# Differential attention's values unit by unit in a shared PSUM bank, short convolutions in halves, three projection groups and their turns moved, filter taps paired: a two-block transformer kernel

## Chip, cores and metric

One core of a Trainium2 chip runs the whole program. The metric is the device time of one execution in microseconds; the kernel before takes 1582.85 us (median of 3 runs, 1582.10 to 1583.59).

## The reference, cut to what matters

Two blocks follow each other on 512 tokens of width 1024. The first has a stick-breaking attention, a pooled and a gated branch and a feed-forward of width 4096. The second, which the change is about, mixes two parts and then has a gated feed-forward (width 2816):

```python
# differential attention, 4 heads, queries 512, keys 256 (context) + 512
s = einsum("bhmqd,bhmkd->bhmqk", q, k) * (64 ** -0.5)      # m: 2 maps of a head
a = softmax(s, axis=-1)
w = a[:, :, 0] - lam * a[:, :, 1]
o = einsum("bhqk,bhkd->bhqd", w, v)                        # then rmsnorm(o) * (1 - lam_init)
# hyena mixer, three parts of width 512: v, x1, x2
u = short_conv(hx @ w_hy)                                  # 3 taps along the tokens
z = v
for n, gate in enumerate((x1, x2)):
    z = gate * (long_conv(z, k_f[:, n]) + skip[n] * z)     # by a transform, a product, its inverse
# the filters k_f: three sine layers of width 64 and one linear layer, once for all tokens
```

## The kernel before, in words

Every product of an activation with a weight is made from split numbers: a value is a high part and a low part in the type fp32r, and three matmuls (high by high, low by high, high by low) stand for one (`mm3`). Weights come in units of 128 x 1024. SP issues their DMAs into four raw buffers, ACT copies a unit to its high part (line 1081), and DVE (line 1651) or, for the units in the list POOL_LOW, POOL (line 2274) subtracts it from the raw values for the low part. Units of the kind "pre" (the transform tables) come already split: POOL issues two DMAs for each (lines 2284, 2285). Small fp32 matmuls have two records each in the trace.

Each engine has one program, written out by hand; it works in its own order and waits on semaphores. The functions with one name on several engines (`diff_turn`, `hyena_turn`, `fold`) are the parts of one step.

**Filters (early, beside the first block's projections).** `filter_layer` makes three sine layers of 64 features; `taps(i, o)` makes two fp32 matmuls with 64 rows of contraction (64 x 512 each, d = 0 and 1), eight times in all; DVE multiplies by the decay, POOL adds and subtracts the two.

**Differential attention.** A unit is one head and 128 queries, 16 units. For unit n:
- PE `diff_scores(n)`: 12 matmuls into banks 0 to 3, two maps side by side on the two halves of the rows.
- DVE `diff_max(n)`: for each map a maximum over 768 keys (line 2062) and a product by -0.125 (line 2064).
- ACT `diff_scores(n)`: for each map the exponential (line 1444), scale 0.125.
- DVE `diff_weights(n)`: reciprocal, factor (line 2074) and the difference of the maps (line 2076).
- PE `diff_turn(n)`: six transposes into banks 4 and 5; ACT copies them to WT (line 1435).
- PE `diff_values(h)`, after the four units of a head: six fp32 matmuls with 512 columns into the free one of banks 6 and 7; ACT evicts O2F (line 1424), DVE then S2F (line 2055), ACT squares it.

Between these PE puts the hyena projections: `hyena_part(j, part)`, 6 matmuls, two parts in each step of the loop, groups j = 0 to 7 into banks 6 and 7 (RING2). ACT writes the convolution's middle tap (`conv_center`, line 1452), DVE adds the other two in six steps (`hyena_conv`, line 2083). In step n PE does scores(n), sometimes values, turn(n-2), two parts.

**Behind it.** PE does turns 0 to 3 of the convolved groups, group 8 with its projection, turns 4 to 7, `sub_sums` (sums of squares for the attention's norm, 16 matmuls of one column, 32 records), group 9 and turn 8. ACT evicts the turns to U (line 1475). `fold(o)` adds and subtracts halves of U (DVE line 2114, high parts ACT line 1481, low parts DVE line 2117 and POOL line 2417). Then for each order o = 0, 1: `forward(o, f)`, f = 0 to 3 (12 matmuls each), `spectral` (DVE: four products at line 2158, then lines 2160 and 2162; ACT the high and POOL the low part), and `backward(o, f)` (12 matmuls each). Turns 9 to 11 and `sub_scale(h)` stand between them. Group 10 stands ahead of backward(0, 2), group 11 after backward(0, 3), beside the gating (DVE lines 2177, 2181), and fold(1) comes next. The forwards take their banks in turn from 0 to 3 (RING4), and a bank is free when its last reader is done. After backward(1, 3) PE starts on w_out_2 (`wide2`) with the attention's half of the input, while ACT and DVE gate and norm the hyena half.

`mm` and `bank` are at lines 431 to 446, PE's loop over the units at about 895 to 935.

## Time and profile before

| what | value |
|---|---|
| median of 3 runs | 1582.85 us |
| the profiled execution | 1580.21 us |
| its span | 1578.5 us |
| PE busy | 1507.5 us (96%), 6878 matmul records |
| DVE busy | 877.3 us (56%) |
| ACT busy | 622.5 us (39%) |
| POOL busy | 291.1 us (18%) |
| mean granted TensorE clock | 0.991 |

The span is the profiled part of the execution; 1.7 us lie around it. A busy time is a share of the whole span and says nothing of a single stage. Matmul records overlap: the time from the start of one to the start of the next is what a matmul costs, and its own duration is longer.

### The profile page before, as it was taken

The page shows a single profiled execution, that of the slowest core. Times are in us where ns is not written, and L with a number is a line of the kernel's source. Part 1 is how long each engine was busy: PE and PEld are TensorE (multiplying, and loading weights), DVE is VectorE, ACT ScalarE, POOL GpSimd, SP SyncE. Part 2 cuts the span into 40 slices and gives each one's busy share as a digit, 9 for nine tenths or more (in the row PEclk, how much of TensorE's full clock was granted, in tenths as well). Part 3 has the DMA queues.
Part 4 walks back from the last instruction along what each step waited for, and adds up shares of the span by engine and source line. Part 5 has one row for each costly group of instructions (what it writes and reads, how often), then busy time and mean ns, then how long its engine had stood idle before and what let it go on. Part 6 is the DMA issues. An engine that isn't in the chain of part 4 may idle for free.

```text
span 1578.5 us, 17718 instructions
## 1 busy us (share of the span) xinstructions
PE 1507.5 (96%) x6878; PEld 1200.0 (76%) x6878; DVE 877.3 (56%) x1429; ACT 622.5 (39%) x978; POOL 291.1 (18%) x289
## 2 busy tenths in 40 slices
PE   6999999999989999999997998989798999999998
PEld 5767667888868878888886876668576888888886
DVE  5445556555467654565447438856766455334534
ACT  5535664222353322334335325644344333223332
POOL 0253111110122200122004310006441110111101
PEclk9999999999999999999999999999999999999999
DMA  7342002654345544545326221124442322323221
GB/s 232 126 146 81 27 28 93 235 166 148 132 134 173 174 147 140 178 145 178 113 100 208 91 67 40 41 94 139 131 154 69 108 93 95 99 89 106 94 94 54
DMA packets 53262, 187.87 MB, mean 119 GB/s; under 512 B 6104, under 2 KB 6616, under 8 KB 52986
## 3 DMA queue, kind: packets, MB, share of 16 engines
q1 hardware_dynamic: 47386, 165.76, 32.3%
q0 software_dynamic: 4736, 16.78, 3.2%
q10 hardware_dynamic: 1056, 4.19, 0.7%
q8 instruction: 55, 0.90, 0.2%
q14 instruction: 29, 0.24, 0.0%
HBM read 174.12 MB, written 12.58 MB: 118 GB/s over the span
## 4 chain that ended last, share of the span: by engine, by line
PE 80%; DVE 9%; issue 4%; ACT 4%; POOL 3%; DMA 0%; SPq 0%; DVEq 0%; POOLq 0%; ACTq 0%
PE PS L447 79%; POOL TMP L2311 2%; DVE smallring L2062 1%; DVE TMP L2083 1%; PE PS L458 1%; ACT em L1444 1%; DVE wl L1651 1%; DVE TMP L2158 1%; DVE em L2076 1%; POOL y L2321 0%; DMA X<-in_x 0%; ACT wh L1081 0%; DVE accm L1631 0%; ACT wt L1435 0%; POOL wl L2274 0%
## 5 line engine op out<-in xcount | busy, mean ns | idle before, releaser
L1651 DVE TENSOR_TENSOR wl<-raw,wh 128x1024 fp32r<-128x1024 f32 x219 | 283.8, 1299 | 283.1 <-ACT wh L1081 283.0
L447 PE MATMUL PS<-HTh,wh 128*128 128x512 f32 x1056 | 419.7, 397 | 12.4 <-DVE TMP L1977 5.8
L447 PE MATMUL PS<-HTh,wl 128*128 128x512 f32 x1056 | 413.0, 391 | 0.0
L447 PE MATMUL PS<-HTl,wh 128*128 128x512 f32 x1056 | 412.8, 391 | 0.0
L1081 ACT ACTIVATE wh<-raw 128x1024 fp32r<-128x1024 f32 x228 | 239.1, 1053 | 286.2 <-PE PS L447 251.9
L447 PEld LDWEIGHTS PS<-HTh,wh 128*128 128x128 f32 x1056 | 199.5, 189 | 61.3 <-issue 11.0
L447 PEld LDWEIGHTS PS<-HTh,wl 128*128 128x128 f32 x1056 | 199.0, 188 | 42.8
L447 PEld LDWEIGHTS PS<-HTl,wh 128*128 128x128 f32 x1056 | 199.5, 189 | 38.5 <-issue 0.5
L447 PE MATMUL PS<-wh,FFh 128*128 128x512 f32 x432 | 169.1, 392 | 0.0
L447 PE MATMUL PS<-wh,FFl 128*128 128x512 f32 x432 | 168.2, 389 | 0.0
L447 PE MATMUL PS<-wl,FFh 128*128 128x512 f32 x432 | 168.1, 389 | 0.0
L1631 DVE SCALAR_TENSOR_TENSOR accm<-raw,small,accm 128x256 f32<-128x256 f32 x224 | 108.0, 516 | 3.4
L2234 DVE SCALAR_TENSOR_TENSOR TMP<-PS,pp,TMP 128x255 f32<-128x255 f32 (+1 forms) x132 | 52.1, 395 | 80.3 <-ACT TMP L1583 76.4
L447 PEld LDWEIGHTS PS<-wh,FFl 128*128 128x128 f32 x432 | 81.1, 188 | 17.1
L447 PEld LDWEIGHTS PS<-wl,FFh 128*128 128x128 f32 x432 | 81.1, 188 | 16.5
L447 PEld LDWEIGHTS PS<-wh,FFh 128*128 128x128 f32 x432 | 81.1, 188 | 16.5
L2384 POOL TENSOR_TENSOR FFl<-TMP,FFh 128x512 fp32r<-128x512 f32 x32 | 41.6, 1299 | 240.1 <-ACT FFh L1295 240.1
L2466 POOL TENSOR_TENSOR FFl<-TMP,FFh 128x512 fp32r<-128x512 f32 x22 | 28.5, 1294 | 211.8 <-ACT FFh L1590 211.8
L1295 ACT ACTIVATE FFh<-TMP 128x512 fp32r<-128x512 f32 x32 | 20.2, 632 | 66.5 <-DVE TMP L1917 66.5
L1291 ACT ACTIVATE TMP<-PS 128x512 f32<-128x512 f32 x32 | 19.0, 595 | 57.7 <-PE PS L447 57.7
L2083 DVE SCALAR_TENSOR_TENSOR TMP<-PS,pp,TMP 128x255 f32<-128x255 f32 (+1 forms) x72 | 28.4, 395 | 16.0 <-ACT TMP L1452 13.9
L2474 POOL TENSOR_TENSOR X<-X,TMP 128x512 f32<-128x512 f32 x14 | 19.7, 1434 | 90.1 <-DVE TMP L2249 90.1
(320 smaller groups left out, 2163.7 us busy)
## 6 DMA issues: line engine op xcount, KB each, us to landing
raw<-in_ws SPq DMA_DIRECT2D x268, 512.0 KB, 3.8
taps<-TMP SPq DMA_DIRECT2D x16, 256.0 KB, 2.5
tab<-in_spec POOLq DMA_DIRECT2D x8, 512.0 KB, 5.6
raw<-taps SPq DMA_DIRECT2D x8, 512.0 KB, 3.7
kd<-TMP POOLq DMA_DIRECT2D x16, 256.0 KB, 4.3
wh<-in_wd POOLq DMA_DIRECT2D x8, 512.0 KB, 3.9
wl<-in_wd POOLq DMA_DIRECT2D x8, 512.0 KB, 4.6
kf<-kd SPq DMA_DIRECT2D x8, 512.0 KB, 3.9
```

The source lines that it names most:

```text
L447: return nc.tensor.matmul(out, l, r, start=start, stop=stop, skip_group_check=True)
L1081: act(WH[u % SLOTS][:, :n], RAW[i % RAWS][:, :n], ACT.Copy).then_inc(sem("w_hi"), 1)
L1291: act(T(q % 2), PS[:, BANK["ff", hf, m], :], ACT.Relu).then_inc(sem("ff_relu"), 1)
L1295: act(FFh[:, m, :], T(2 + q % 2), ACT.Copy).then_inc(sem("ff_hi"), 1)
L1631: stt(acc, r[:, k % 4, :], c, acc, ALU.mult, ALU.add).then_inc(sem("mod_acc"), 1)
L1651: tt(WL[k][:, :n], RAW[RAW_AT["unit", u, 0] % RAWS][:, :n], f32(WH[k][:, :n]), ALU.subtract).then_inc(sem("lo_dve"), 1)
L2083: stt(out[:, do], ps[:, di], pp("hy_conv_w_2", 12 * w + j), out[:, do], ALU.mult, ALU.add).then_inc(sem("hc_v"), 1)
L2234: stt(z[:, do], ps[:, di], pp("ffn_conv_w_2", 22 * w + m), z[:, do], ALU.mult, ALU.add).then_inc(sem("uc_v"), 1)
L2311: tt(T(k), T(3), T(5), op).then_inc(sem("tap_ed"), 1)
L2384: tt(FFl[:, q % 16, :], T(2 + q % 2), f32(FFh[:, q % 16, :]), ALU.subtract).then_inc(sem("ff_lo"), 1)
L2466: tt(FFl[:, m - first_m, :], T(m % 4), f32(FFh[:, m - first_m, :]), ALU.subtract).then_inc(sem("ug_lo"), 1)
L2474: tt(x, x, T(4 + q % 4), ALU.add).then_inc(sem("dn_xp"), 1)
```

## The change

Nine edits; the diff is cut to its core.
1. PE's taps go in pairs: the filter layers put their 64 features out twice, on partitions 0 to 63 and 64 to 127, w4 is stored as 128 x 1024, and the matmul for d = 1 uses the upper half of the rows.
2. The scale 0.125 moves into q (ACT's high part, DVE's low part), and the maximum is negated by its own instruction; line 2064's 32 instructions go.
3. The attention's values are made per unit, 6 matmuls of 128 columns into columns 256 to 383 of bank 5, the upper one of the transposes' banks; ACT and DVE evict 128 columns, 16 times. The turn of a unit moves one step earlier, and WT has two buffers.
4. `hyena_conv` is done in two halves of three steps, one in each step of the loop.
5. The low parts of the weight units from the fourth hyena group on go to POOL.
6. The turns of groups 0 to 6 stand around the last unit's turn and ahead of its values, turn 7 after them.
7. Group 8 (with its turn) moves behind forward(0, 3), groups 9 and 10 behind backward(0, 3), group 11 between backward(1, 1) and backward(1, 2), its turn after backward(1, 3), before `wide2`.
8. `sub_sums` moves behind forward(0, 0), sub_scale(0) behind forward(0, 1).
9. ACT's eviction of turn 8 (and 11) stands ahead of its two copies of the backward sums.

```diff
-BEFORE = 10
+BEFORE = 8
...
-        if o == 0:
-            pack(colmajor("w_in_2", 1536 + 10 * P, 1))
+        pack(colmajor("w_in_2", 1536 + (8 if o == 0 else 11) * P, 1))
         pack(inv[2] + inv[3], "pre")
         if o == 0:
-            pack(colmajor("w_in_2", 1536 + 11 * P, 1))
+            pack(colmajor("w_in_2", 1536 + 9 * P, 2))
...
 POOL_LOW = [u for u in range(NU) if u not in PRE and (
-    AT["dft_f", 0, 0][0][0] + SLOTS - 1 <= u < AT["w_out_2", 0, 0][0][0] + SLOTS - 1
+    AT["w_in_2", 0, 1536][0][0] + SLOTS - 1 <= u < AT["w_out_2", 0, 0][0][0] + SLOTS - 1
...
+                for d in range(2):
+                    pr = slice(64 * d, 64 * d + 64)
+                    mm(PS[:, BANK["tap", n + d], :], TMP[pr, 4, i * P:(i + 1) * P], W4[pr, o * S:(o + 1) * S], True,
+                       True).then_inc(sem("p_tap"), 1)
...
-            def diff_values(h):
-                b = bank(("dv", h), "dv_ev", h + 1, (13 - BANK["hy", (ahead - 1) // 4],))
+            def diff_values(n):
+                h, _ = DIFF[n]
+                BANK["dv", n] = b = TPAIR[0] + 1
                 e.wait_ge("v2_ev", 3)
                 e.wait_ge("v2_evv", 3)
-                e.wait_ge("wt_ev", 4 * h + 4)
+                e.wait_ge("wt_ev", n + 1)
+                drained[b] = ("dv_ev", n + 1)
                 for k in range(6):
-                    i = mm(PS[:, b, :], V2[:, k, h * P:(h + 1) * P], WT[:, k, :], k == 0, k == 5)
+                    i = mm(PS[:, b, 256:384], V2[:, k, h * P:(h + 1) * P], WT[n % 2][:, k, :], k == 0, k == 5)
...
+            for n in range(len(DIFF) + 1):
+                if n < len(DIFF):
+                    diff_scores(n)
+                else:
+                    for j in TURN_AT[0]:
+                        hyena_turn(j)
+                if n:
+                    diff_turn(n - 1)
+                if n < len(DIFF):
+                    for part in range(2):
+                        hyena_part(n // 2, n % 2 * 2 + part)
+                else:
+                    for j in TURN_AT[1]:
+                        hyena_turn(j)
+                if n:
+                    diff_values(n - 1)
+            hyena_turn(7)
...
             for o in range(2):
                 for f in range(4):
                     forward(o, f)
-                    if f == 0:
-                        if o:
-                            hyena_turn(10)
+                    if f == 0 and o == 0:
+                        sub_sums()
+                    if f == 1 - o:
                         sub_scale(3 * o)
-                    if f == 3:
-                        hyena_turn(9 + 2 * o)
-                        if o == 0:
-                            sub_scale(1)
+                    if f == 3 and o == 0:
+                        sub_scale(1)
+                    if f in (1, 2) and o:
+                        hyena_turn(8 + f)
                     if f >= 2:
                         backward(o, f - 2)
-                if o == 0:
-                    hyena_group(10)
+                hyena_group(8 + 3 * o)
                 backward(o, 2)
                 backward(o, 3)
+                hyena_turn(8 + 3 * o)
                 if o == 0:
-                    hyena_group(11)
+                    hyena_group(9)
+                    hyena_group(10)
                     sub_scale(2)
...
+            for n in range(len(DIFF) + 1):      # VectorE
                 if n < len(DIFF):
                     diff_max(n)
+                if n > 1:
+                    if n < len(DIFF):
+                        hyena_conv(n // 2 - 1, range(3 * (n % 2), 3 * (n % 2) + 3))
+                    else:
+                        hyena_conv(7)
+                        fold(0, (0, 1))
                 if n < len(DIFF):
                     diff_weights(n)
+                    weights(unit("w_in_2", 0, 1536 + n // 2 * P) + SLOTS - 1)
+                if n:
+                    diff_values(n - 1)
...
+            for n in range(len(DIFF) + 1):      # ScalarE
+                if n > 1:
+                    diff_values(n - 2)
+                if n == len(DIFF):
+                    for j in TURN_AT[0]:
+                        hyena_turn(j)
+                if n:
+                    diff_turn(n - 1)
+                if n < len(DIFF):
+                    diff_scores(n, 0)
+                    diff_scores(n, 1)
...
+            diff_values(len(DIFF) - 1)
```

In order 1 VectorE does hyena_conv(10) behind spectral(4) and sub_high(3), ahead of spectral(5); hyena_conv(8) and hyena_conv(11) stand ahead of its wait for the last backward, hyena_conv(9) behind fold(1) and sub_high(2).

## Rows read from the trace of the kernel before

**Rows 1.** Windows: us, busy (records) of PE, PEld, DVE, ACT, POOL, clock, DMA
```profile
60.00:130.00 70.00, 70.00 (x272) 49.72 (x272) 32.36 (x37) 27.49 (x36) 35.64 (x31) 1.00 0.45 141
950.11:1057.21 107.10, 95.53 (x504) 68.26 (x505) 81.67 (x166) 56.19 (x97) 1.13 (x2) 1.00 0.18 55
1106.86:1129.34 22.48, 12.99 (x46) 7.56 (x44) 17.73 (x31) 6.71 (x13) 7.78 (x8) 0.90 0.45 145
1129.34:1153.43 24.09, 21.04 (x89) 16.99 (x89) 17.12 (x21) 9.30 (x14) 18.63 (x12) 0.95 0.28 88
```

**Rows 2.** Waits of PE, 950 to 1160: releaser, us in total, times, longest
```profile
PE PS L447 <- ACT em L1444: 7.8, 9, 1.0
```

**Rows 3.** Timeline of PE, one unit: start, us, instructions
```profile
993.23 0.50 PE L447 MATMUL PS<-KTh,QTh 64*128 64x512 f32 x2
994.48 0.87 PE L458 MATMUL PS<-cst,em 128*128 128x128 f32 x6
995.11 0.48 PE L447 MATMUL PS<-HTh,wh 128*128 128x512 f32 x1
...
998.10 0.50 PE L447 MATMUL PS<-KTh,QTh 64*128 64x512 f32 x2
```

**Rows 4.** Groups of DVE by line: busy us, mean ns of one
```profile
L2062 DVE TENSOR_REDUCE smallring<-PS 128x1 f32<-128x768 f32 x32 | 30.4, 951 | 0.0
L2064 DVE TENSOR_SCALAR smallring<-smallring 128x1 f32<-128x1 f32 x32 | 4.9, 154 | 1.1
L2076 DVE SCALAR_TENSOR_TENSOR em<-em,smallring,em 128x768 f32<-128x768 f32 x16 | 16.3, 1019 | 0.6
```

**Rows 5.** Timeline of DVE, one low part and one whole convolution
```profile
953.59 1.21 DVE L1651 TENSOR_TENSOR wl<-raw,wh 128x1024 fp32r<-128x1024 f32 x1
958.30 2.54 DVE L2083 SCALAR_TENSOR_TENSOR TMP<-PS,pp,TMP 128x255 f32<-128x255 f32 x6
```

**Rows 6.** Timeline of PE, a head's values and the turn behind them
```profile
977.55 5.42 PE L447 MATMUL PS<-wt,V 128*128 128x512 f32 x12
982.81 0.82 PE L458 MATMUL PS<-cst,em 128*128 128x128 f32 x6
```

**Rows 7.** Timeline of PE, fp32 matmuls of 1 and of 128 columns
```profile
1066.22 3.63 PE L447 MATMUL PS<-cst,s2f 128*128 128x1 f32 x32
144.66 1.09 PE L447 MATMUL PS<-wst,bc 128*64 128x128 f32 x16
```

**Rows 8.** Groups of ACT by line: busy us, mean ns of one
```profile
L1444 ACT ACTIVATE em<-PS,smallring 128x768 f32<-128x768 f32 x32 | 28.6, 901 | 6.6 <-DVE smallring L2064 6.3
L1435 ACT ACTIVATE wt<-PS 128x768 f32<-128x768 f32 x16 | 12.9, 809 | 17.4 <-PE PS L458 17.4
L1487 ACT ACTIVATE ndg<-cst,small 128x128 f32<-128x128 f32 x16 | 5.1, 390 | 0.0
```

**Rows 9.** Timeline: POOL's low part of a unit and DVE beside it
```profile
1139.82 2.84 POOL L2274 TENSOR_TENSOR wl<-raw,wh 128x1024 fp32r<-128x1024 f32 x1
...
1140.33 2.88 DVE L2162 TENSOR_TENSOR TMP<-TMP 128x512 f32<-128x512 f32 x1
```

**Rows 10.** Timeline of PE, 1107 to 1130: the stretch behind the first gating
```profile
1115.12 0.47 PE L447 MATMUL PS<-EDh,wh 128*128 128x512 f32 x1 [1.80 <-issue]
1126.95 2.07 PE L447 MATMUL PS<-ndg,cst 128*128 128x512 f32 x2 [5.01 <-DVE TMP L2083]
1129.34 0.79 PE L447 MATMUL PS<-EDh,wh 128*128 128x512 f32 x1 [0.32 <-DVE TMP L2158]
```

**Rows 11.** Windows of 1 us: the clock behind sub_sums and behind the gap
```profile
1072.00:1073.00 1.00, 1.00 (x4) 0.80 (x3) 0.00 (x0) 0.00 (x0) 0.00 (x0) 0.50 0.77 193
1127.00:1128.00 1.00, 1.00 (x2) 0.45 (x2) 1.00 (x2) 0.00 (x0) 0.00 (x0) 0.50 1.13 410
```

**Rows 12.** Timeline of PE: a step of four tap records and what follows
```profile
65.16 1.98 PE L447 MATMUL PS<-w,TMP 64*128 64x512 f32 x4
67.07 0.50 PE L447 MATMUL PS<-HTh,wh 128*128 128x512 f32 x1
```

More of the change, by code:

```diff
@@ L919, in hyena_part @@
                     i.then_inc(sem("p_hy"), 1)
[L921 to L932 removed]
             RING4, ACC = (0, 1, 2, 3), (4, 5, 6, 7)
             def hyena_group(j):
[L938 removed]
+                bank(("hy", j), "hc_v", 6 * j + 6, ACC if j == 10 else RING4)
                 for k in KT:
@@ L1385, in rotated @@
                 dh = QTh[:, r, :] if r < 4 else KTh[:, r - 4, 256:]
-                act(dh, T(2 + r % 3), ACT.Copy).then_inc(sem("qk2_hi"), 1)
+                act(dh, T(2 + r % 3), ACT.Copy, **({"scale": 0.125} if r < 4 else {})).then_inc(sem("qk2_hi"), 1)
             for m in range(4):
@@ L1492, in sub_high @@
                 act(O2h[:, h, :], NO2[:, :], ACT.Copy).then_inc(sem("o2_hi"), 1)
[L1494 to L1495 removed]
             fold(0)
[L1497 to L1506 removed]
+            diff_squares(3)
+            hyena_turn(7)
             def spectral(n):
@@ L1518, in scalar_program @@
                     spectral(4 * o + f)
-                    if f == 0:
-                        if o:
-                            hyena_turn(10)
+                    if f == 0 and o == 0:
+                        e.wait_ge("sub_v", 4)
+                        act(SUBR[:, 16:32], SUBR[:, 16:32], ACT.Sqrt, scale=2.0 ** -8,
+                            bias=1e-6 * 2.0 ** -8).then_inc(sem("sub_rt"), 1)
+                        sub_diag(0)
+                    if f == 1 - o:
                         sub_high(3 * o)
@@ L2050, in vector_program, with fold, fold_low, diff_values @@
             ts(SUBG, pp("subln_2"), 1.0 - lam_init, None, ALU.mult).then_inc(sem("lam_v"), 1)
-            def diff_values(h):
-                e.wait_ge("dv_o", h + 1)
-                ts(S2F[:, h, :], PS[:, BANK["dv", h], :], 2.0 ** 64, -2.0 ** 64, ALU.min, ALU.max).then_inc(sem("dv_ev"), 1)
+            def fold(o, cs):
+                for c in cs:
+                    i = c % 2
+                    if o == 0:
+                        e.wait_ge("u_ev", 4)
+                        e.wait_ge("p_ht", c + 3)
+                    else:
+                        for t in (i, i + 2):
+                            e.wait_ge(*Z_READY(0, t))
+                        e.wait_ge("z_p", 1)
+                    tt(T(2 + c), U[:, i, 0:512], U[:, i + 2, 0:512], ALU.add if c < 2 else ALU.subtract).then_inc(sem("fd_v"), 1)
+            def fold_low(o, c):
+                e.wait_ge("ed_hi", 4 * o + c + 1)
+                tt(EDl[:, c, :], T(2 + c), f32(EDh[:, c, :]), ALU.subtract).then_inc(sem("ed_lo"), 1)
+            def diff_values(n):
+                h, qb = DIFF[n]
+                e.wait_ge("dv_o", n + 1)
+                ts(S2F[:, h, qb * P:(qb + 1) * P], PS[:, BANK["dv", n], 256:384], 2.0 ** 64, -2.0 ** 64, ALU.min,
+                   ALU.max).then_inc(sem("dv_ev"), 1)
             def diff_max(n):
@@ L2119, in sub_high, with spectral @@
+                if n:
+                    diff_values(n - 1)
             def sub_high(h):
                 e.wait_ge("p_sn", h + 1)
-                e.wait_ge("dv_o", h + 1)
+                e.wait_ge("dv_o", 4 * h + 4)
                 e.wait_ge("o2_lo", h)
                 tt(NO2[:, :], O2F[:, h, :], PS[:, BANK["sn", h], :], ALU.mult).then_inc(sem("sn_v"), 1)
-            fold(0)
-            weights(unit("w_in_2", 0, 1536 + 8 * P) + SLOTS - 1)
-            hyena_conv(8)
+            def spectral(n):
+                kf = KF[n % 2]
+                br, bi = PS[:, BANK["fw", n, 0], :], PS[:, BANK["fw", n, 1], :]
+                k0, k2 = 2 + 2 * (n % 2), 3 + 2 * (n % 2)
+                e.wait_ge("p_fw", n + 1)
+                e.wait_ge(f"d_kf{n % 2}", 16 * (n // 2 + 1))
+                if n >= 2:
+                    e.wait_ge("ys_lo", 2 * (n - 2) + 2)
+                e.wait_ge("pr_v", 6 * n)
+                for k, x, c in ((k0, br, 0), (6, bi, 1), (k2, br, 1), (7, bi, 0)):
+                    tt(T(k), x, kf[:, c, :], ALU.mult).then_inc(sem("pr_v"), 1)
+                e.wait_ge("pr_v", 6 * n + 2)
+                tt(T(k0), T(k0), T(6), ALU.subtract).then_inc(sem("pr_v"), 1)
+                e.wait_ge("pr_v", 6 * n + 4)
+                tt(T(k2), T(k2), T(7), ALU.add).then_inc(sem("pr_v"), 1)
@@ L2129, in vector_program @@
+            fold_low(0, 0)
+            fold(0, (2, 3))
+            fold_low(0, 2)
+            spectral(0)
             ps, fits, r, q = PS[:, BANK["sub"], 0:16], SUBR[:, 0:16], SUBR[:, 16:32], SUBR[:, 32:48]
```

235 lines of the change are left out of this document (78 added, 157 removed).

## The prediction

> **What bounds the kernel now.** I read the windows by stage first. From 60 to 130 us PE is busy without a break, although POOL and DVE work beside it; there a microsecond less of PE is a microsecond less of time. The differential attention (950.11 to 1057.21) has 107.1 us and 95.5 of PE, and the stretch from the first gating to the last backward has 22.5 us with 13.0 of PE and 24.1 with 21.0 [rows 1]. So 11.6 + 9.5 + 3.1 = 24.2 us of PE are idle in the part that is rebuilt, and this is all that a new order alone can bring.
>
> What PE waits for in the attention is ACT's exponential, 9 times, about 1 us each [rows 2]. The cause lies one engine back. A unit without values costs PE 998.10 - 993.23 = 4.87 us: scores 1.25, turn 0.63, two projection parts 2.99 [rows 3]. DVE's unit is longer: two maxima and two scalings 2 x (0.95 + 0.15) = 2.2, reciprocal, factor and difference about 1.5 (1.02 the difference) [rows 4], half a convolution 1.27 and half a low part 0.6 [rows 5], together 5.5 to 5.6. DVE sets the pace for three units, and in the fourth PE is alone for 982.81 - 977.55 = 5.26 us with a head's values [rows 6] while DVE has no work. The two limits add up instead of covering each other.
>
> Behind the gating PE starts forward(1, 0) at 1115.12, waits 5.01 us for a convolution, and reaches forward(1, 1) only at 1129.34 [rows 10].
>
> **The sum, part by part**, against the profiled 1580.2 us (2.6 below the median of 1582.85).
>
> *Taps.* A step has four records of 0.43 and takes PE 67.07 - 65.16 = 1.91 us [rows 12]. Two matmuls on different halves of the rows can run side by side, as the two maps' scores do (rows of x2, [rows 3]), but the two records of one fp32 matmul use the same rows. In the order A, A, B, B only the second A and the first B overlap: three slots for four, 8 x 0.43 = 3.4 us. Bounds: 0 (no overlap) and 6.9 (both overlap). I take 3.4. The doubled features change no column count, so the filter layers cost nothing more; POOL's tap chain has slack beside PE [rows 1].
>
> *Values.* Before: 4 x 5.26 = 21.0. After: 16 x 12 records of 128 columns. With one column a record costs 3.63 / 32 = 0.113 us, the pace of loading 128 weight columns; at 512 columns it costs 0.43, so 128 columns stream in 0.107 [rows 6, 7]. If load and stream overlap, a record costs 0.115 and a unit 1.4, with the change of shape 1.5: 24.0, so 3.0 more than before. Bounds: 0.107 and, one after the other, 0.22. I take 0.115, because the 12 records at 0.43 show their loads wholly hidden.
>
> *Pace of a unit.* PE: 4.87 + 1.5 = 6.37 us. DVE: maxima 1.9 (negation costs nothing), 1.5, half a convolution 1.27, a small eviction 0.3, no low part: 5.0. ACT: 0.81 + 2 x (0.90 + 0.20) + half of 0.77 and of 1.05 + 0.39 = 4.3 [rows 8]. The ring scores, maximum, exponential, exponential, scores is 1.25 + 0.1 + 0.96 + 0.95 + 1.1 + 0.2, about 4.6, and the ring from a turn by the copy of WT, two exponentials and the weighting to the next turn about 5.2. All are under 6.37, so PE runs through. The tightest place: turn(n) may not write bank 5 before DVE has evicted values(n-1), PE's last work of the step before. That takes 0.2 + 0.4 + 0.3 + 0.1 = 1.0 us, and scores(n) cover 1.25. First wait as before (0.5), then 949.85 + 6.75 + 14 x 6.37: step 16 starts at 1045.8.
>
> *From there to backward(0, 3).* Turns, the last turn and values need 5.85 us. fold(0) then is bare, for group 8 no longer covers it: ACT evicts seven turns and one unit first, and the last low part is ready 11.8 later, so forward(0, 0) ends at +12.4, 3.8 of that idle. Then sub_sums 3.6, three forwards and four backwards 7 x 2.75, two sub_scale 1.9, group 8 5.5, and about 2 us in which sub_scale(0) waits for the norm's chain (DVE, ACT's root, ACT's diagonal), now begun behind spectral(0): +45.1, 1090.9. DVE's work of spectral(0), 3.9, is hidden by sub_sums and forward(0, 1).
>
> *Order 1.* ACT evicts turn 8 first, so gating and fold(1) are 1.1 later; groups 9 and 10 (11 us) fill what was idle. forward(1, 0) ends at +14.8, sub_scale(3) at +16.1. Then banks and DVE decide: forward(1, 1) gets the banks of group 9 and of forward(1, 0), and waits 0.8 for spectral(4); forward(1, 2) gets one of forward(1, 1), and spectral(5) stands behind sub_high(3) and convolution 10 (0.7 + 2.54), so it waits 3.6 more. Then two forwards, four backwards and group 11 run through: +47.0, 1137.9, and turn 11 0.5: `wide2` starts at 1138.4 and not at 1153.4, **15.0 us earlier**. Its own cover of 10.9 us is longer than the gating and norm behind it, 1.1 later.
>
> *Clock.* It falls to 0.50, the 1.2 GHz level, behind sub_sums and behind the gap in order 1 [rows 11]; eight matmuls at 0.43 for 0.23 in the first case. Sparse stretches stay (turns, bare fold, sub_sums, the wait before forward(1, 2)). I take 2 us; bounds 0 and 5.
>
> *The rest.* q's scale is in operations that are there; the later low parts lie on an idle POOL; the DMAs keep their order; each pre unit is issued over 4 us ahead of its use.
>
> Sum: 3.4 + 15.0 - 2 = 16.4 us. 1580.2 - 16.4 = 1563.8 for the profiled execution, **1566.4 for the median**.
>
> **Rules against it.** The 12 value records on the full array, 0.43 us apart for 512 columns, leave no room for a load between them [rows 6]. The Trainium skill (TensorE: Matmul & The Clock Gate, The mechanism) says that a weight load overlaps running matmuls only where the row group differs; these records all use the whole array, so by the rule their loads would lie bare. By that rule (rival 1) the time is 1587; the rows speak against it.
>
> POOL's low part at 1139.82 lasts 2.84 us, and a DVE subtraction issued at 1140.33 takes 2.88 [rows 9]. The Trainium skill (SBUF — State Buffer, Who interferes with whom) says that a DVE instruction with two SBUF inputs and a GpSimd instruction that reads SBUF shut each other out for the whole instruction. The trace agrees; this is rival 4.
>
> **Rivals.**
> 1. *The value records pay load and stream one after the other*, 0.113 + 0.107 = 0.22: 192 x 0.105 = 20.2 us more, 1586.6, slower than before. Place: the end of each unit on PE. For it: nothing in the trace has fp32 records of 128 columns over 128 weight columns back to back. Against it: 16 records of 128 columns and 64 weight columns in 1.09 us, 0.054 apart, two column halves at a time [rows 7]. It decides from 0.20 a record (16.4 / 192 = 0.085 over 0.115). 5%.
> 2. *The shared bank sets the pace.* If ACT or DVE is 1 us late with the eviction of values(n-1), each turn stalls: 15 us over 15 units, 1581, no change. For it: the margin is 0.25 us; against it: both have over 1 us of free time in each unit. 7%.
> 3. *The moved groups leave as much bare as they cover.* Fold and norm chain cost 5 more in order 0, spectral(4) to (6) 3 more in order 1: 1574. For it: a chain over four engines, scheduled by hand from single rows. 11%.
> 4. *POOL's port.* Five low parts (2.4 each) now lie beside DVE's difference of the maps, which has two SBUF inputs. If POOL starts first, turn(n) is late by 2.4 less 1.2 of slack, five times 1.2: 6 us, 1572. Against it: POOL waits for ACT's copy (1.05), which starts with DVE's own release, so DVE comes first. 9%.
>
> **How the numbers follow.** My forecast has 68%. About 0.2% (3.2 us) is what a measurement can tell from no change. Faster: 68 + 11 + 9 = 88%; same: rival 2, 7%; slower: rival 1, 5%. Range: lower end with full overlap of the taps (-3.5), no clock loss (-2) and half of the 9 us of remaining waits gone (-4): 1557; upper end takes in rivals 3 and 4 and no gain from the taps: 1576.
>
> **What would show it.** Value records 0.11 to 0.12 us apart; about 6.4 us from scores to scores; no line 2064; PE's waits for line 1444 gone except at the start. A pace over 6.8 with DVE's S2F eviction as releaser is rival 2, records at 0.22 rival 1. Four tap records in about 1.5 us. `wide2` some 18 us earlier, PE idle about 4 us ahead of forward(0, 0) and about 4 ahead of forward(1, 2)'s second half. If the attention, without the turns put into it, does not get shorter by some 9 us, or the stretch behind it by 5, the forecast is wrong there.

## The result and the profile after

The kernel after takes **1556.42 us** (median of 4 runs, 1555.44 to 1558.83), the kernel before 1582.59 us beside it (4 runs, 1582.1 to 1583.59): a ratio of 0.9836, 95% interval 0.9821 to 0.985. I had forecast 1566.4 with a range of 1557 to 1576. The sign and the places were right; the time lies 10 us under the forecast and 0.6 under the range. The profiled execution took 1555.44 us with a span of 1553.7, against 1578.5 before: 24.8 us less where I had summed 16.4.

The page of the kernel after: busy time of each engine, and the groups of low parts on POOL and on DVE.

```profile
PE 1501.7 (97%) x7022; PEld 1211.4 (78%) x7022; DVE 866.1 (56%) x1402; ACT 626.1 (40%) x990; POOL 307.7 (20%) x296
...
L1658 DVE TENSOR_TENSOR wl<-raw,wh 128x1024 fp32r<-128x1024 f32 x212 | 274.4, 1299 | 282.4 <-ACT wh L1087 282.1
L2287 POOL TENSOR_TENSOR wl<-raw,wh 128x1024 fp32r<-128x1024 f32 x16 | 40.2, 2512 | 114.1 <-ACT wh L1087 114.1
```

PE is busy 5.8 us less than before with 144 records more, the 192 value records of 128 columns for 48 of 512. Against 24.8 us of span that is a quarter: the rest was idle time. POOL's line 2287 has 16 low parts of 128 x 1024, against 9 before.

The waits of PE from 950 to 1160 in the kernel after, as [rows 2] (releaser, us in total, times, longest).

```profile
PE PS L448 <- DVE TMP L2147: 3.6, 2, 3.2
PE PS L448 <- issue: 2.0, 2, 1.3
PE PS L448 <- DVE no L2134: 1.3, 2, 0.9
PE PS L448 <- DVE EDl L2076: 1.1, 1, 1.1
```

The exponential's line is gone from that list. The timeline of PE in the kernel after: a step of taps, as [rows 12]; a unit, as [rows 3]; the last unit's end and the fold; order 1 up to `wide2`, as [rows 10].

```profile
63.31 1.13 PE L448 MATMUL PS<-w,TMP 64*128 64x512 f32 x4
64.37 0.50 PE L448 MATMUL PS<-HTh,wh 128*128 128x512 f32 x1
...
937.97 0.49 PE L448 MATMUL PS<-KTh,QTh 64*128 64x512 f32 x2 [1.98 <-DVE V L2045]
...
955.26 0.50 PE L448 MATMUL PS<-KTh,QTh 64*128 64x512 f32 x2
...
957.13 0.48 PE L448 MATMUL PS<-HTh,wh 128*128 128x512 f32 x1
...
959.95 1.50 PE L448 MATMUL PS<-wt,V 128*128 128x128 f32 x12
961.38 0.50 PE L448 MATMUL PS<-KTh,QTh 64*128 64x512 f32 x2
...
1034.72 1.47 PE L459 MATMUL PS<-cst,TMP 128*128 128x128 f32 x12
...
1041.69 0.47 PE L448 MATMUL PS<-EDh,wh 128*128 128x512 f32 x1 [1.32 <-issue]
...
1044.83 0.47 PE L448 MATMUL PS<-EDh,wh 128*128 128x512 f32 x1 [1.07 <-DVE EDl L2076]
...
1105.25 0.79 PE L448 MATMUL PS<-EDh,wh 128*128 128x512 f32 x1 [3.18 <-DVE TMP L2147]
...
1129.10 0.47 PE L448 MATMUL PS<-wh,O2h 128*128 128x512 f32 x1 [0.73 <-issue]
```

The four tap records take 64.37 - 63.31 = 1.06 us, where they took 1.91. The attention starts at 937.97, 7.1 us earlier than before (945.03); eight steps of 0.85 are 6.8 of it. A unit takes 961.38 - 955.26 = 6.12 us, values included. `wide2` starts at 1129.10, 24.3 us earlier than before (1153.43). So nearly all of the gain lies ahead of `wide2`. The windows of the stretches in the kernel after, as [rows 1] (us, busy time and records of PE, PEld, DVE, ACT, POOL, granted clock, DMA).

```profile
937.97:1034.72 96.75, 96.09 (x654) 82.14 (x655) 72.42 (x142) 59.12 (x111) 16.10 (x9) 1.00 0.19 61
1034.72:1079.35 44.63, 41.30 (x208) 33.07 (x207) 32.97 (x54) 23.14 (x44) 25.97 (x21) 0.96 0.39 122
1079.35:1129.10 49.75, 44.47 (x189) 34.76 (x188) 34.05 (x57) 19.03 (x32) 29.70 (x23) 0.97 0.46 153
```

In the attention (the first row) PE is idle for 0.7 us of 96.8; in the two stretches behind it for 3.3 and 5.3 us.

### The profile page after: what moved, and what is told of

It is laid out like the page before. It is cut to its first block, busy times and chain, and to the rows that moved or that the text cites. A ratio compares the mean times of both kernels' runs of the same rounds, so it can differ in the third digit from the quotient of the medians.

```text
span 1553.7 us, 18006 instructions
## 1 busy us (share of the span) xinstructions
PE 1501.7 (97%) x7022; PEld 1211.4 (78%) x7022; DVE 866.1 (56%) x1402; ACT 626.1 (40%) x990; POOL 307.7 (20%) x296
## 4 chain that ended last, share of the span: by engine, by line
PE 86%; DVE 5%; issue 3%; POOL 3%; ACT 2%; DMA 0%; SPq 0%; POOLq 0%; DVEq 0%; ACTq 0%
PE PS L448 85%; PE PS L459 2%; POOL TMP L2324 2%; DVE wl L1658 1%; DVE TMP L2147 0%; POOL y L2334 0%; DVE TMP L1711 0%; DMA X<-in_x 0%; ACT wh L1087 0%; DVE accm L1638 0%; DVE HTl L1974 0%; DVE TMP L2110 0%; ACT TMP L1367 0%; DVE Y L1863 0%; DVE TMP L1904 0%
## 5 line engine op out<-in xcount | busy, mean ns | idle before, releaser
L1658 DVE TENSOR_TENSOR wl<-raw,wh 128x1024 fp32r<-128x1024 f32 x212 | 274.4, 1299 | 282.4 <-ACT wh L1087 282.1
L2247 DVE SCALAR_TENSOR_TENSOR TMP<-PS,pp,TMP 128x255 f32<-128x255 f32 (+1 forms) x132 | 52.1, 395 | 79.3 <-ACT TMP L1590 75.4
L2287 POOL TENSOR_TENSOR wl<-raw,wh 128x1024 fp32r<-128x1024 f32 x16 | 40.2, 2512 | 114.1 <-ACT wh L1087 114.1
```

What stands on the lines that cost most here:

```text
L1658: tt(WL[k][:, :n], RAW[RAW_AT["unit", u, 0] % RAWS][:, :n], f32(WH[k][:, :n]), ALU.subtract).then_inc(sem("lo_dve"), 1)
L2247: stt(z[:, do], ps[:, di], pp("ffn_conv_w_2", 22 * w + m), z[:, do], ALU.mult, ALU.add).then_inc(sem("uc_v"), 1)
L2287: tt(WL[k][:, :n], RAW[RAW_AT["unit", u, 0] % RAWS][:, :n], f32(WH[k][:, :n]), ALU.subtract).then_inc(sem("lo_pool"), 1)
```

## The experiments

The groups e1 to e4; e5, e6, f1, f2; f3, g1, g2, h1; k0 to k3; and m1, m2 each shared a chip and its runs of the kernel before; ratios are to those. The unchanged kernel after gave medians of 1556.42, 1555.87 and 1558.03 on three occasions, and in the profiled executions of k0 to k3, m1 and m2 the attention started anywhere from 937.5 to 941.4, with the same code ahead of it. Differences of under 3 us are therefore read from a stretch of the trace, not from the medians. Two stretches serve: from the first scores to step 16, the step behind the last scores (96.75 us in the kernel after), and from step 16 to `wide2` (94.38).

**The taps alone (e1), and everything but the taps (e2).** e1 is the kernel before with edit 1, e2 the kernel after without it.

```diff
+                for d in range(2):
+                    pr = slice(64 * d, 64 * d + 64)
+                    mm(PS[:, BANK["tap", n + d], :], TMP[pr, 4, i * P:(i + 1) * P], W4[pr, o * S:(o + 1) * S], True, True)
```

> Edit 1 alone on the kernel before: the two taps of a step stand on the two halves of the rows, nothing else changed. Theory 1 (drawn from the profile after, where four tap records end in 1.13 us and the attention starts 7.1 us earlier): both records of one matmul run beside both of the other, two slots for four, so 8 steps x 2 x 0.43 = 6.9 us less than the kernel before: a ratio of 0.9956. Rival (the prediction's own term): only the second record of the first and the first of the second overlap, 3.4 us less, 0.9978. Second rival: the tap chain on the vector and GpSimd engines sets the pace there, 0 to 2 us less.

> The kernel after without edit 1: taps one after the other on the upper 64 rows, the rest of the change left in. Theory 1: the parts add up, so the time is that of the kernel after plus 6.9 us, 1563.3, a ratio of 0.9878 to the kernel before, and the attention and what is behind it account for the other 19 us. Rival: the parts share a bound (the saving before the attention is partly eaten by a later wait), then it is above after by 3.4 or less (1559.8, 0.9856).

e1: 1573.99 us, a ratio of 0.9957 (0.994 to 0.9974), 6.8 us by the ratio. e2: 1564.74, 0.9893 (0.9878 to 0.9907), and its span is 1561.6, 7.9 us over the kernel after. A step of e1 on PE:

```profile
63.76 1.13 PE L447 MATMUL PS<-w,TMP 64*128 64x512 f32 x4
64.81 0.50 PE L447 MATMUL PS<-HTh,wh 128*128 128x512 f32 x1
```

1.05 us for four records of 512 columns, two slots of 0.43 and the change of shape (before, 1.91 for four slots and it): not three slots. The parts add up. My term of 3.4 was half of what the taps bring.

**Value records twice (e5).** The kernel after with each unit's six value matmuls issued twice into one accumulation.

```diff
-                for k in range(6):
+                for k in [*range(6), *range(6)]:
```

> The kernel after, with each unit's value matmuls issued twice into the same accumulation (12 more records of 128 columns a unit; the attention's output is then doubled, so the outputs differ from the reference's). Theory 1: the tensor engine alone sets the pace, and a record costs 0.113 to 0.12 us, load and stream overlapped: 192 x 0.115 = 22 us more than the kernel after (1578.5, 0.9974). Rival (the prediction's rival 1, load and stream one after the other) 0.22 each, 42 us more (1598.5, 1.010). Third: other engines' slack is what sets the pace and takes part of it up, under 18 us more.

1579.19 us, 0.9976 (0.9966 to 0.9986), 22.8 us over 1556.42. Two units on PE:

```profile
958.30 0.50 PE L448 MATMUL PS<-KTh,QTh 64*128 64x512 f32 x2
...
963.03 2.84 PE L448 MATMUL PS<-wt,V 128*128 128x128 f32 x24
965.80 0.50 PE L448 MATMUL PS<-KTh,QTh 64*128 64x512 f32 x2
```

A unit takes 7.50 us and not 6.12: 1.38 / 12 = 0.115 us a record, and no other engine takes any of it up. Load and stream one after the other would have been 0.22. Rival 1 of the prediction is out, and PE alone sets the pace of the attention.

**Convolutions whole (e4), low parts back on DVE (e3), both (g1).** Edits 4 and 5 undone in the kernel after, singly and together.

```diff
-                        hyena_conv(n // 2 - 1, range(3 * (n % 2), 3 * (n % 2) + 3))
+                        if n % 2 == 0:
+                            hyena_conv(n // 2 - 1)
...
-    AT["w_in_2", 0, 1536][0][0] + SLOTS - 1 <= u < AT["w_out_2", 0, 0][0][0] + SLOTS - 1
+    AT["dft_f", 0, 0][0][0] + SLOTS - 1 <= u < AT["w_out_2", 0, 0][0][0] + SLOTS - 1
```

> The kernel after, with the low parts of the weights that ride in the attention subtracted on the vector engine again, as in the kernel before (five or so of them, 1.2 us each). Theory 1: the vector engine has 70 us of work in the 92 us of the attention, and 6 more leave it under the tensor engine's pace; only the eviction that the next unit's turn waits for comes late, some 0.55 us in four or five units, so 2.7 us more than the kernel after (1559.1, 0.9852). Rival A: the queue hides it, 0 to 0.5 us more. Rival B (the prediction's rival 4, the port shared by GpSimd and the vector engine): the moved low parts cost the kernel after something, and undoing the move gains 1 to 6 us.

> The kernel after, with each short convolution of the attention whole in every second unit (2.54 us on the vector engine at once) and not in halves of 1.27 in each. Theory 1: a unit with a whole convolution has 6.3 us of work for the vector engine and the next one 3.8; the tensor engine's 6.12 is passed only just, and the turn that waits for the eviction is late by 0.4 us in seven units: 2.8 us more than the kernel after (1559.2, 0.9852). Rival: the slack of the queue takes it up, 0 to 0.5 us more.

> The kernel after with both: convolutions whole in every second unit, and the low parts of the weights of the attention on the vector engine. e4 (whole convolutions alone) took 9 us more than the kernel after, where 2.8 were expected; in its trace four differences of the maps last 2.9 us and not 1.02, each while GpSimd makes a low part, and the next turn waits 1.8 us. Theory 1: what costs the 9 us is that the longer convolution puts the difference behind GpSimd's start; with the low parts on the vector engine the four waits of 1.8 go, and what is left is the work of 6.3 us in the units with a convolution: 1 to 3 us more than after (1558.5, 0.9848). Rival: it is the vector engine's amount of work that costs, then this kernel, with 1.2 us more of it in every second unit, is slower than e4: 1566 or more (0.990).

e3: 1557.67 us, 0.9846 (0.9831 to 0.9861), 1.3 over the kernel after and within what separates its own measurements; in its trace four turns wait 0.9 us in all for line 2082, and those four units take 6.44 to 6.46 us. e4: 1565.42, 0.9895 (0.988 to 0.991), 9.0 over. g1: 1562.71, 0.9871 (0.9852 to 0.9891), 6.3 over. From the first scores to step 16 the traces have:

| convolutions | low parts on POOL | low parts on DVE |
|---|---|---|
| in halves | 96.75 (after) | 98.41 (e3) |
| whole | 104.19 (e4) | 101.18 (g1) |

So e4 was a miss by a factor of three, and g1, with more work for DVE than e4, is 3.0 us shorter. The cause stands in DVE's timeline. First a unit of the kernel after with POOL's low part beside it, then one of e4 with DVE, POOL and PE.

```profile
954.41 1.02 DVE L2102 SCALAR_TENSOR_TENSOR em<-em,smallring,em 128x768 f32<-128x768 f32 x1
...
954.89 2.78 POOL L2287 TENSOR_TENSOR wl<-raw,wh 128x1024 fp32r<-128x1024 f32 x1 [8.53 <-ACT wh L1087]
```

```profile
966.61 2.54 DVE L2110 SCALAR_TENSOR_TENSOR TMP<-PS,pp,TMP 128x255 f32<-128x255 f32 x6
...
969.27 2.37 POOL L2288 TENSOR_TENSOR wl<-raw,wh 128x1024 fp32r<-128x1024 f32 x1 [11.74 <-ACT wh L1087]
969.57 2.89 DVE L2102 SCALAR_TENSOR_TENSOR em<-em,smallring,em 128x768 f32<-128x768 f32 x1
...
972.71 0.87 PE L459 MATMUL PS<-cst,em 128*128 128x128 f32 x6 [1.76 <-DVE s2f L2082]
```

In the kernel after DVE starts the difference of the maps at 954.41, POOL its low part at 954.89; DVE takes 1.02 us, POOL 2.78 where it takes 2.39 alone. In e4 the longer convolution lets POOL start first, by 0.30 us, and the difference takes 2.89. The next turn waits 1.76 for what DVE does behind it. That happens four times, 7.0 us of waits. In g1 POOL is out of it and four units are 7.22 to 7.25 us long instead of 6.12, those in which a whole convolution (2.54) and a low part (1.2) fall together: 4.1 us of waits, with no low part on POOL beside them. The Trainium skill (SBUF — State Buffer, Who interferes with whom) says that the two instructions shut each other out for their whole length; the trace agrees to within 0.2 us: in e4 the difference ends 0.82 us behind POOL's low part (972.46 and 971.64) and alone takes 1.02. What it means for this change: with convolutions in halves moving the low parts to POOL gains 1.7 us, with whole ones it costs 3.0. The halves keep the difference 0.48 us ahead of POOL.

**The two DVE edits on the kernel before (e6), one of them alone (g2).** e6: edits 2 and 5; g2: edit 2.

```diff
-                    nc.vector.reduce_max(r[:, m:m + 1], s, axis=mybir.AxisListType.X).then_inc(sem("df_mx"), 1)
-                    e.wait_ge("df_mx", 4 * n + 2 * m + 1)
-                    ts(r[:, m:m + 1], r[:, m:m + 1], -0.125, None, ALU.mult).then_inc(sem("df_mx"), 1)
+                    nc.vector.reduce_max(r[:, m:m + 1], s, axis=mybir.AxisListType.X, negate=True).then_inc(sem("df_mx"), 1)
```

> The kernel before with two of the small edits alone: the scaling by -0.125 taken out of the vector engine (the negation in the maximum, the scale in q's split) and the low parts of the weights moved to GpSimd. The values stay with each head. Theory 1: the vector engine's pace was what made the tensor engine wait for the exponentials; its unit falls from 5.5 to about 4.7 us, under the tensor engine's 4.87, so the waits for line 1444 (7.8 us) go and the attention is 7 to 9 us shorter: 1574.5, a ratio of 0.9949. Rival: the waits come back elsewhere (the ring of exponential and scores), 0 to 3 us less, and the placing of the values unit by unit is what brings the attention's gain.

> The kernel before with the scaling by -0.125 taken out of the vector engine alone; the low parts stay on the vector engine. e6 (both) took 9 us more than before: its differences last 2.9 us four times behind GpSimd's low parts, and the tensor engine waits 2.1 us for the exponential behind each. Theory 1: the low parts on GpSimd are the whole of that loss, and the scaling alone brings 0.3 us of the vector engine's time a unit where it sets the pace, 12 units: 1 to 4 us less than before (1579.5, 0.998). Rival: the vector engine isn't what the tensor engine waits for; the same time as before within 0.5 us. Second rival: the denser pace lets the granted clock fall, more than before.

e6: 1591.72 us, 1.0057 (1.0042 to 1.0073): 9 us slower than before, where I expected 8 less. g2: 1578.73, 0.9978 (0.9965 to 0.9991), 3.4 us less. e6 on POOL, DVE and PE:

```profile
972.93 2.39 POOL L2275 TENSOR_TENSOR wl<-raw,wh 128x1024 fp32r<-128x1024 f32 x1 [9.49 <-ACT wh L1081]
973.23 2.91 DVE L2077 SCALAR_TENSOR_TENSOR em<-em,smallring,em 128x768 f32<-128x768 f32 x1
...
979.05 0.58 PE L447 MATMUL PS<-KTh,QTh 64*128 64x512 f32 x2 [2.15 <-ACT em L1444]
...
981.06 6.24 PE L447 MATMUL PS<-wt,V 128*128 128x512 f32 x12
987.13 0.82 PE L458 MATMUL PS<-cst,em 128*128 128x128 f32 x6
```

The same meeting. From the first scores to the turns behind the last values e6 has 121.8 us, the kernel before 112.2. Its whole convolutions put the difference behind POOL's low part in four units, PE's waits for the exponential come to 11.2 us in place of 7.8, and behind the 2.15 us of idle time the granted clock falls (0.83 over 978 to 988): the head's values take 6.07 us and not 5.26. g2 shows that DVE did set the pace before: with 0.3 us less a unit the waits for the exponential fall from 7.8 to 4.0 us. (The profiled execution of g2, 1582.70, is the longest of its ten, so nothing else is read from it.)

**Banks of `wide2` one by one (f1).**

```diff
-            banks0 = [bank(("o2", i), "o2_v", i + 1, RING4) for i in range(4)]
+            banks0 = []
...
+                        if c == 0:
+                            banks.append(bank(("o2", i), "o2_v", i + 1, RING4))
```

> The kernel after, with the output projection (wide2) taking its four banks one by one, each just before its first matmul, and not all four ahead of the first. Theory 1: the 0.73 us idle ahead of it is the wait for the eviction of turn 11, whose bank is one of the four; taken last, it is out of the way: 0.8 to 1.0 us less than the kernel after (1555.5). Rival: that idle time is the issue of the first matmul and stays, 0.

1554.95 us, 0.9829 (0.9805 to 0.9853). From the last step of the attention to `wide2` its trace has 1128.47 - 1035.11 = 93.36 us, the kernel after 1129.10 - 1034.72 = 94.38: 1.0 less, and the 0.73 us of "issue" are gone. They were the wait for ACT's eviction of turn 11.

**Convolution 10 later (f2).**

```diff
-                    if f == 0 and o:
+                    if f == 1 and o:
                         hyena_conv(10)
```

> The kernel after, with convolution 10 behind spectral(5) on the vector engine, and turn 10 behind backward(1, 0) on the tensor engine. Theory 1: the wait of 3.18 us ahead of forward(1, 2)'s second half is for spectral(5), which stands behind convolution 10 in the vector engine's queue; moved, the wait goes and the bank is free 2.5 us earlier: 2.5 to 3 us less than the kernel after (1553.6, 0.9817). Rival: the tensor engine then waits for convolution 10 itself ahead of turn 10, 0 to 1 us less.

1558.45 us, 0.9848 (0.9827 to 0.9868), 95.55 us from step 16 to `wide2` against 94.38: nothing gained. PE in f2:

```profile
1105.24 0.50 PE L448 MATMUL PS<-EDh,wh 128*128 128x512 f32 x1 [0.74 <-DVE TMP L2149]
...
1109.97 0.47 PE L448 MATMUL PS<-ysh,wh 128*128 128x512 f32 x1 [3.07 <-POOL ysl L2447]
```

The wait ahead of forward(1, 2) falls from 3.18 to 0.74 us and one of 3.07 stands ahead of backward(1, 0). The releaser named is POOL's low part of spectral(5), which backward(1, 0) does not read. By the code it is the bank: group 10 is in the ring of backward's four banks, so backward(1, 0) needs convolution 10, which ends at 1109.7 there. Either order waits for the same sum of DVE's work. That the bank holds it is read from the code and these two ends, and was not tested.

**`sub_sums` into the fold's wait (f3).**

```diff
+            sub_sums()
             for o in range(2):
                 for f in range(4):
                     forward(o, f)
-                    if f == 0 and o == 0:
-                        sub_sums()
```

> The kernel after, with sub_sums put ahead of forward(0, 0), into the wait for the fold's low part, the squares of the last head between the fold's high parts on ScalarE, and the norm's chain of small operations ahead of spectral(0). Theory 1: sub_sums (3.5 us) covers the waits of the fold on the tensor engine (1.3 and 1.1 us idle) and the norm's chain is ready before sub_scale(0) asks for it (0.24 us): 2 us less than the kernel after (1554.4, 0.9822). Rival: sub_sums needs the last head's squares, which come only behind the fold's high parts, so the wait is longer ahead of sub_sums instead: 0 to 1 us more than after.

The diff above shows PE's part; on DVE the norm's chain also goes ahead of spectral(0). 1559.09 us, 0.985 (0.9834 to 0.9866), 2.7 over the kernel after, and 97.75 us from step 16 to `wide2`, 3.4 more. PE in f3:

```profile
1042.47 5.43 PE L448 MATMUL PS<-cst,s2f 128*128 128x1 f32 x32 [1.58 <-ACT s2f L1435]
...
1057.99 2.05 PE L448 MATMUL PS<-ndg,cst 128*128 128x512 f32 x2 [2.96 <-ACT ndg L1498]
```

It waits 1.58 us for the last head's squares, its 32 records take 5.43 us and not 3.63 (the granted clock is 0.66 over them, 1.00 in the kernel after), and sub_scale(0) waits 2.96 for the diagonal, which on ACT stands behind spectral(0)'s high parts, now later. The first wait is the rival's mechanism. The low clock and the longer wait, which the move of the norm's chain on DVE brings, were in neither theory.

**Low parts and the spectrum's DMA in order 1 (h1, k2), the fold's low part (k1).** h1 and k2 take POOL's low part at 1096.19 out of DVE's chain; k2 also puts one DMA ahead of another on SP, and sub_low(3) on POOL one spectral step later; k1 moves one low part of each fold from POOL to DVE. The diff has h1's condition first, then k2's edits on POOL and SP, then k1's.

```diff
-                    weights(unit("dft_f", 128, f * P, o) + SLOTS - 1)
+                    if o == 0 or f > 1:
+                        weights(unit("dft_f", 128, f * P, o) + SLOTS - 1)
...
-                    weights(unit("dft_f", 128, f * P, o) + SLOTS - 1)
+                    if n != 4:
+                        weights(unit("dft_f", 128, f * P, o) + SLOTS - 1)
...
-                    if f == 0:
+                    if n in (0, 5):
                         sub_low(3 * o)
...
+                if n == 4:
+                    load_spectrum(6)
                 weights(unit("dft_f", 128, f * P, o) + SLOTS - 1)
-                if n + 2 < 8:
+                if n + 2 < 8 and n != 4:
...
             fold_low(0, 0)
+            fold_low(0, 1)
             fold(0, (2, 3))
```

> The kernel after, with one low part of order 1 (the unit of group 11, 2.4 us on GpSimd at 1096.2, used at 1116.9) done behind the low parts of spectral(5) instead of ahead of those of spectral(4). In the kernel after the vector engine's subtraction at 1097.2 takes 1.92 us beside it and not 0.68, and the vector engine works without a break from there to spectral(5), for which forward(1, 2) waits 3.2 us. Theory 1: the subtraction is back at 0.68 and the wait is 1.2 us shorter: 1.2 us less than the kernel after (1555.2, 0.9827). Rival: another GpSimd operation then meets the vector engine's chain, 0 to 0.5 us less.

> The kernel after, with the low part of group 11's unit behind the low parts of spectral(4) on GpSimd, as in h1, but only by one place, and with the DMA of the spectrum for spectral(6) issued ahead of the raw unit's on SP. In h1 the vector engine waited 13.3 us for that spectrum: its DMA was issued at 1114.67 and not at 1099.00, behind the raw unit's, which waits for the low part that frees its buffer. Theory 1: that queue was the whole of h1's loss; now it is away, and the subtraction of spectral(4) is back at 0.68 us: 1.2 us less than the kernel after. Rival A: the raw unit itself comes late, 2 us or more above after. Rival B: the same as after, another engine ends that stretch.

> The kernel after, with the second low part of each fold made by the vector engine itself (0.6 us) and not by GpSimd, beside which the vector engine's next sums of the fold take 2.39 us for two and not 1.29. Theory 1: shut out for 1.1 us, it gets 0.5 us back in each fold; the tensor engine's wait of 1.07 us for the third low part of the fold falls to 0.5, and order 1 starts 0.5 us earlier: 0.5 to 1.0 us less than the kernel after. Rival: no meeting of the two engines, the sums are slow for another reason; then 0.6 us more in each fold, 0.6 to 1.2 us more than after.

h1: 1568.74 us, 0.9906 (0.9888 to 0.9924), 12 us over the kernel after. DVE and SP in h1:

```profile
1101.30 0.68 DVE L2149 TENSOR_TENSOR TMP<-TMP 128x512 f32<-128x512 f32 x1
...
1114.67 0.91 SPq L2592 DMA_DIRECT2D kf<-kd  x2
...
1122.52 2.48 DVE L2147 TENSOR_TENSOR TMP<-PS,kf 128x512 f32<-128x512 f32 x4 [13.29 <-DMA kf<-kd]
```

The subtraction is back at 0.68 us, as expected, and 13.29 us are lost to a queue that I had not followed: the low part frees a raw buffer, SP waits for that buffer to load the next unit, and the spectrum's DMA stands behind that load. In k2 it stands ahead of it (issued at 1097.00): 1555.45 us, 0.9833 (0.9818 to 0.9847), and 1127.61 - 1034.39 = 93.22 us from step 16 to `wide2`, 1.2 less than the kernel after. k1: 1554.78, 0.9832 (0.9817 to 0.9847), 1127.95 - 1034.20 = 93.75 us, 0.6 less; the two sums of the fold take 1.29 us and not 2.39.

**All three with f1's (k3, m1), beside the kernel after (k0, m2).**

> The kernel after, unchanged, on the same chip as the next three, so that differences of a few us can be read: 1556.4 by the first measurement, within 1.5 us by every theory.

> The kernel after with the edits of f1 (banks taken one by one, 0.8), k1 (0.5 to 1.0) and k2 (1.2) together. Theory 1: they lie one behind the other on the path and add up, 2.5 to 3 us less than the kernel after run beside it. Rival: the edits of the fold are covered by the wait in order 1, 1 to 2 us less.

> k3's kernel again. Theory 1: f1, k1 and k2 shortened the stretch from the last unit's turn to wide2 by 1.0, 0.6 and 1.2 us in their traces (94.4 us in the kernel after), so at an equal clock it has 91.6 here, and the time is 2 to 3 us under the kernel after run beside it. Rival: the clock gives part of it back, as in k3's profiled execution, 0 to 2 us less.

> The kernel after once more, beside m1: 1556 within 1.5 us, and 94.4 us from step 16 to wide2 in its trace.

k3 1554.01 us (0.982, 0.9806 to 0.9833) beside k0 1555.87 (0.9838, 0.9824 to 0.9853); m1 1555.15 (0.9828, 0.9815 to 0.9841) beside m2 1558.03 (0.9846, 0.9832 to 0.9859). First m1, then m2 on PE, step 16 and `wide2`:

```profile
1037.62 1.47 PE L459 MATMUL PS<-cst,TMP 128*128 128x128 f32 x12
...
1129.36 0.48 PE L448 MATMUL PS<-wh,O2h 128*128 128x512 f32 x1
```

```profile
1038.10 1.47 PE L459 MATMUL PS<-cst,TMP 128*128 128x128 f32 x12
...
1133.92 0.47 PE L448 MATMUL PS<-wh,O2h 128*128 128x512 f32 x1 [0.73 <-issue]
```

m1 has 91.7 us where 91.6 were expected; m2 has 95.8, 1.4 more than the first trace of the same kernel, in a run with a mean granted clock of 0.989 and not 0.991. k3's trace does not show the gain: 94.2 us, against 94.4 in k0. It is of k3's slowest execution (1558.22), with a granted clock of 0.93 in that stretch. At one and the same clock in it, 0.96, the two kernels compare at 94.4 (the first trace and k0) and 91.7 (m1), 2.6 us. By the medians the version with the three edits was 1.9 and 2.9 us faster side by side, with intervals that overlap in each pair.

## Why the prediction was right and wrong

Against the profiled execution I had summed 16.4 us and 24.8 came. By stretch:

| step of the prediction | forecast | measured | more gained |
|---|---|---|---|
| taps | 3.4 | 7.1 (eight steps: 6.8) | +3.7 |
| first scores to step 16 | 100.8 | 96.75 | +4.0 |
| step 16 to backward(0, 3)'s end, at full clock | 45.1 | 43.1 | +2.0 |
| from there to `wide2`, at full clock | 47.5 | 48.2 | -0.7 |
| loss at the lower clock in both | -2 | -3.1 | -1.1 |
| behind `wide2` | 0 | 0.5 shorter | +0.5 |

The loss at the lower clock is read from PE's timeline: behind `sub_sums` eight records of 512 columns stand 0.43 us apart and not 0.23 (granted clock 0.50, the 1.2 GHz level), 1.6 us; behind the wait of 3.18 us in order 1 six records and a turn cost 1.5 us more than at full clock. Only edits 1, 4 and 5 were undone in the kernel after. What edits 2, 3 and 6 to 9 bring there is read from the stretches and not tested one by one (edit 2 was tested on the kernel before, g2).

**Failed: the taps' term.** I wrote that "the two records of one fp32 matmul use the same rows. In the order A, A, B, B only the second A and the first B overlap". Four records cost 1.06 us: both records of one matmul run beside both of the other. [rows 3] show a pair of single records on the two halves side by side; for matmuls of two records no row of before did, and between 0 and 6.9 I took the middle, by an argument on the order of the records and by no row.

**Failed: the unit's pace.** I took 4.87 us for a unit without values and 1.5 for the values. The parts now measure scores 1.24, turn 0.63, projection 2.82 and values 1.43: 6.12. The projection's 2.99 of [rows 3] was not all the projection's. In the kernel before, the last record of the projections and the scores behind it, and for comparison the last record ahead of a step of taps:

```profile
997.70 0.39 PE L447 MATMUL PS<-HTh,wl 128*128 128x512 f32 x1
998.10 0.50 PE L447 MATMUL PS<-KTh,QTh 64*128 64x512 f32 x2
```

```profile
64.84 0.39 PE L447 MATMUL PS<-HTh,wl 128*128 128x512 f32 x1
65.16 1.98 PE L447 MATMUL PS<-w,TMP 64*128 64x512 f32 x4
```

Records of one shape start 0.23 us apart. The change from 128 rows to 64 makes it 0.32 ahead of the taps, where PE waits for nothing, and ahead of the scores it is 0.40. So of the 0.17 some 0.09 is the change of shape, which the sum had a second time in the 1.5 for the values, and some 0.08 is left. I take it for a wait for the exponential that the timeline doesn't print, because PEld's list of waits in the kernel before has 15 for the exponential and PE's has 9; that was not tested. The values' 1.43 for 1.5 is the rest. Fourteen units were 3.6 us shorter than forecast, the two steps ahead of them 0.4. So a duration read off a unit may hold more than the step's own work, and a change of shape belongs to a pair of neighbours: it goes away when another step is put between them.

**Failed: a wait and a loss that cover each other.** The sum had about 2 us in which sub_scale(0) waits for the norm's chain, and beside it the lower clock behind `sub_sums`. The wait measures 0.24 us. The slow records are those of forward(0, 1), right ahead of sub_scale(0), and their 1.6 us pass while DVE and ACT work on the chain. Without them PE would come 1.6 us earlier and wait about 1.8 (an estimate from this timeline, not tested). That is nearly all of the 2.0 in the third row. (The terms that the prediction names for that stretch add up to 44.7, not 45.1.)

**The range.** Its lower end put in the full taps, no clock loss and 4 us of waits, 9.5 in all, but held the pace of a unit at 6.37 as if it were known. Each unit's part was a reading with an error of 0.05 to 0.2, times fourteen. With that bound the range would have held the time.

**Held.** That PE was idle for want of DVE in three units and had the values alone in the fourth: the waits for line 1444 are gone behind the first unit, and g2 shows DVE's part. The value record: 0.115 taken, 0.115 measured by e5, against which the Trainium skill's rule (TensorE: Matmul & The Clock Gate, The mechanism) that a load overlaps only with another row group would have given 1587; the measurement decides against it for these records. (The same section of the Trainium skill also lets a load into the background weight buffer go ahead of running matmuls; no run here shows which buffer a load went to.) The wait of some 3.6 us ahead of forward(1, 2)'s second half for spectral(5) behind convolution 10: 3.18, and 0.43 ahead of forward(1, 1), where 0.8 was forecast. PE idle ahead of forward(0, 0) and inside it: 2.8 us for 3.8.

**Missed places.** PE waits 0.94 us ahead of forward(1, 2)'s first half for DVE's line 2134, and `wide2` takes four banks at once and one is turn 11's: 1.0 us (f1). With them the waits of order 1 are 5.3 us and not 4.4, which is the fourth row. The granted clock fell to 0.50 behind the wait of 3.18 (window 1106 to 1107), and forward(1, 2)'s second half runs at 0.43 us a record; this and the fall behind `sub_sums` are the places that the prediction named, and its 2 us for them was 1.1 too little.

**Rivals.** 1 is out by e5. 2 (the shared bank sets the pace) is out in this kernel, PE waits 0.4 us in the attention for line 1451 and 0.2 for 2102; but its margin is real: e3, e4 and g1 show the very wait, for line 2082, as soon as DVE is late. 4 (POOL's port) didn't happen, for the reason that I gave, DVE comes first; the price I gave it, 1.2 us a meeting, was too low: 1.8 us in e4. 3 (the moved groups leave as much bare as they cover) didn't happen either: the two stretches behind the attention have 94.4 us, and the forecast was 92.6 and 2 for the clock.

## What to carry to other kernels

Before two instructions that can shut each other out are put side by side, ask which starts first and by how much: here 0.48 us of lead are worth 7.4 us of the attention (e4), and the edit that makes the lead (halves of a convolution) looks like mere balancing. Follow a step that is moved through every queue behind what it frees: a low part moved behind two other steps on POOL held up a raw buffer, with it SP, and with it a DMA that had nothing to do with either. A per-unit duration that is multiplied by the number of units needs a bound of its own. And ask of every two losses in a sum whether they pass at the same time.

## What was not expected of the hardware

- Two fp32 matmuls with 64 rows each on the two halves of the rows, both as two records of 512 columns: the four records take 1.05 us, against 1.91 on one half.
- A meeting of POOL's subtraction of 128 x 1024 with DVE's instruction with two SBUF inputs costs the later one up to 1.9 us; DVE's comes to 2.9 us in place of 1.02 if POOL is first, POOL's to 2.78 in place of 2.39 if DVE is first by 0.48.
- `sub_sums`' 32 records of one column: 3.63 us in the kernel after, 5.43 in f3, where the same records stood behind 1.58 us of idle time; the granted clock over them was 0.66 and not 1.00.
